# Weight columns taken 512 at a time in two projections, and a first chunk with its rounded products first

## The reference

```python
# first block, each of 2 layers
x = x + 0.5 * swiglu(rms_norm(x, ffn1_norm[l]), ffn1_w_gate[l], ffn1_w_up[l], ffn1_w_down[l])
h = rms_norm(x, mix_norm[l])
(nq, ..., wv, bgate) = jnp.split(h @ w_in[l], SPLIT_POINTS, axis=-1)     # 1024 x 5656
g = jax.nn.sigmoid(bgate).reshape(B, S, 3, D_MODEL)                      # last 3072 columns
merged = g[:, :, 0] * (y_nsa @ w_up_nsa[l]) + g[:, :, 1] * (y_sb @ w_up_sb[l]) + g[:, :, 2] * (y_swa @ w_up_swa[l])
# second block, each of 2 layers
q, k, v, r, a_low, u, v_sgu = split_proj(x @ w_in[l])                    # 1024 x 2576
```

## Time and profile before

| | |
|---|---|
| median of 3 runs | 2310.48 us (2309.97 to 2311.44) |
| the profiled execution | 2309.98 us |
| its span, first to last instruction | 2308.1 us |
| mean granted clock of PE | 0.994 |
| PE busy | 2266.3 us, 98% |
| DVE busy | 1599.9 us, 69% |
| ACT busy | 1243.4 us, 54% |

### The profile page before, as it was taken

One profiled execution on the slowest core, in us unless ns is written; L12 is line 12 of the kernel. 1 busy time (PEld: TensorE's weight loads), 2 busy tenths in 40 slices (PEclk: granted clock), 3 DMA queues, 4 the chain that ended last, 5 costly groups with the idle time before them and its releaser, 6 DMA issues.

```text
span 2308.1 us, 31674 instructions
## 1 busy us (share of the span) xinstructions
PE 2266.3 (98%) x13500; PEld 1971.8 (85%) x13500; DVE 1599.9 (69%) x1552; ACT 1243.4 (54%) x1272; POOL 48.1 (2%) x67
## 2 busy tenths in 40 slices
PE   8999999999999999999999999999999999899998
PEld 7888989788888899997888999888888998788886
DVE  6765845777477558557774656688887666688887
ACT  4434644454354346444443545577776545477775
POOL 1000100000000000000000000000000000000000
PEclk9999999999999999999999999999999999899999
DMA  7755443555556554535555554599998554599995
GB/s 229 219 190 170 143 148 129 164 183 192 191 172 193 182 165 134 159 132 182 183 189 191 171 177 165 178 341 348 369 345 278 180 183 148 193 346 344 348 367 188
DMA packets 309953, 490.96 MB, mean 213 GB/s; under 512 B 15504, under 2 KB 205120, under 8 KB 309808
## 3 DMA queue, kind: packets, MB, share of 16 engines
q1 hardware_dynamic: 305712, 475.35, 61.2%
q0 software_dynamic: 3104, 10.38, 1.6%
q10 hardware_dynamic: 992, 3.15, 0.4%
HBM read 487.40 MB, written 1.44 MB: 212 GB/s over the span
## 4 chain that ended last, share of the span: by engine, by line
PE 93%; DVE 4%; ACT 2%; issue 1%; DMA 0%; DVEq 0%; SPq 0%; ACTq 0%
PE PS L687 20%; PE PS L688 20%; PE PS L691 20%; PE PS L764 14%; PE PS L767 7%; PE PS L1388 1%; PE PS L991 1%; PE PS L956 1%; ACT RH L1557 1%; DVE RL L2057 1%; PE PS L930 1%; PE PS L941 1%; DVE X L2442 1%; PE PS L1353 1%; PE PS L1409 1%
## 5 line engine op out<-in xcount | busy, mean ns | idle before, releaser
L2057 DVE TENSOR_TENSOR RL<-RINGS,RH 128x2048 fp32r<-128x2048 f32 x448 | 1017.5, 2273 | 475.0 <-ACT RH L1557 472.5
L1557 ACT ACTIVATE RH<-RINGS 128x2048 fp32r<-128x2048 f32 x447 | 849.0, 1900 | 464.2 <-PE PS L691 449.5
L687 PE MATMUL PS<-RH,HTS 128*128 128x256 f32 (+1 forms) x1696 | 547.6, 334 | 0.4 <-DVE HTS L2039 0.4
L688 PE MATMUL PS<-RH,HTS 128*128 128x256 f32 (+1 forms) x1696 | 537.2, 328 | 0.0
L764 PE MATMUL PS<-HTS,RH 128*128 128x512 f32 x1384 | 416.8, 397 | 1.5 <-DVE HTS L2043 1.3
L691 PE MATMUL PS<-RL,HTS 128*128 128x256 f32 (+1 forms) x1696 | 400.9, 327 | 0.0
L687 PEld LDWEIGHTS PS<-RH,HTS 128*128 128x128 f32 x1696 | 319.8, 189 | 32.7 <-issue 2.5
L688 PEld LDWEIGHTS PS<-RH,HTS 128*128 128x128 f32 x1696 | 321.0, 189 | 27.9
L691 PEld LDWEIGHTS PS<-RL,HTS 128*128 128x128 f32 x1696 | 290.3, 189 | 31.1 <-DVE RL L2057 0.4
L764 PEld LDWEIGHTS PS<-HTS,RH 128*128 128x128 f32 x1384 | 248.6, 188 | 49.3 <-issue 1.6
L767 PE MATMUL PS<-HTS,RL 128*128 128x256 f32 x1408 | 285.4, 282 | 1.4 <-DVE RL L2057 1.4
(11 more groups left out here) (441 smaller groups left out, 2529.0 us busy)
## 6 DMA issues: line engine op xcount, KB each, us to landing
RINGS<-w_in SPq DMA_DIRECT2D x64, 1024.0 KB, 5.4
RINGS<-w_gate SPq DMA_DIRECT2D x64, 1024.0 KB, 5.4
RINGS<-w_up SPq DMA_DIRECT2D x64, 1024.0 KB, 5.6
RINGS<-w_down SPq DMA_DIRECT2D x64, 1024.0 KB, 5.4
RINGS<-ffn_w_up SPq DMA_DIRECT2D x44, 1024.0 KB, 5.4
RINGS<-ffn_w_down SPq DMA_DIRECT2D x44, 1024.0 KB, 4.9
RINGS<-ffn_w_gate SPq DMA_DIRECT2D x43, 1024.0 KB, 5.4
RINGS<-w_out SPq DMA_DIRECT2D x16, 1024.0 KB, 4.9
```

The costliest lines, as they stand in the source:

```text
L687: mm(dst, a_[0], b_[0], start=start, stop=False)
L688: mm(dst, a_[0], b_[1], start=False, stop=False) if left else mm(dst, a_[1], b_[0], start=False, stop=False)
L1557: A(splits.buffer(RH, RH3)[:, 0:width], RINGS[:, slot, 0:width], ACT.Copy).then_inc(wh_ready, 1)
L2057: TTn(RL[:, slot, 0:width], RINGS[:, slot, 0:width], splits.buffer(RH, RH3)[:, 0:width].bitcast(F32), ALU.subtract).then_inc(wl_ready, 1)
```

## The change

- Chunks 11 to 22 of the first mixer become six pairs. A load of a pair has four of the eight blocks of rows and 512 columns; the two loads of a pair add up in PSUM, half t = 1 of the rows in bank 1, half t = 0 in bank 0. Each load has 24 products of 512 columns (`to_wide_rows`), t = 1 first. ACT takes bank 0 in turn i when the pair is complete (even i), DVE bank 1 in the same turn, after a new semaphore `chunk_half` that PE raises when t = 1 of the second load is complete.
- Units 1 to 10 of the second block become five pairs in the same way.
- PE waits for bank 1 before the first load of a pair, and for bank 0 in the middle of it.
- In the first chunk of all, both parts' products with rounded weights (k = 0 to 6) come ahead of the wait for RL.

```diff
             for l in range(L):
                 swiglu(l, "ffn1")
                 for j in range(N1):
-                    cols(a["w_in"], l, OFF1[j], W1[j])
+                    if j < WIDE:
+                        cols(a["w_in"], l, OFF1[j], W1[j])
+                    else:
+                        half, c0 = (j - WIDE) % 2, OFF1[j - (j - WIDE) % 2]
+                        src = a["w_in"][l].rearrange("(k p) n -> p k n", p=P)[:, 4 * half:4 * half + 4, c0:c0 + 512]
+                        load(src, lambda r: r.rearrange("p (k n) -> p k n", n=512))
...
                         rounded_with_both(0, k)
+                    if opening:
+                        for k in range(K - 1):
+                            rounded_with_both(1, k)
                     pe.wait_ge(wl_ready, splits.v + splits.n)
                     for k in range(K):
                         rest_with_rounded(0, k)
                     rounded_with_both(0, K - 1)
+                if opening:
+                    for k in range(K):
+                        rest_with_rounded(1, k)
+                    rounded_with_both(1, K - 1).then_inc(chunks_done, 1)
+                    return
...
+            def to_wide_rows(half, lhs, between=None):
+
+                def items(wh, wl):
+                    wh, wl = (w.rearrange("p (k n) -> p k n", n=512) for w in (wh, wl))
+                    return [(PS[:, t, :], tuple(x[:, 4 * half + k, t * P:(t + 1) * P] for x in lhs), (wh[:, k, :], wl[:, k, :]),
+                             half + k == 0, half == 1 and k == 3, False) for t in (1, 0) for k in range(4)]
+                split_products(SLOT, 4, items, half=chunk_half if half else None, between=between)
...
                 for j in range(N1):
                     if j == 11:
                         pe.wait_ge(ng_cols, l + 1)
-                    elif j >= 2:
+                    elif j >= 2 and (j < WIDE or (j - WIDE) % 2 == 0):
                         col_taken(j - 2)
...
+                    elif (j - WIDE) % 2 == 0:
+                        to_wide_rows(0, HT, between=lambda: col_taken(j - 1))
                     else:
+                        to_wide_rows(1, HT, between=(lambda: transpose_y(tr1(l, 2), rows_src(0, l), 2)) if j == N1 - 1 else None)
...
                 def unit(i):
 
-                    if 2 <= i < 15:
+                    if i in (3, 5, 7, 9) or N2 <= i < 15:
                         taken(i - 2)
...
+                        elif i % 2:
+                            to_wide_rows(0, HT, between=(lambda: taken(i - 1)) if i > 1 else None)
                         else:
-                            to_rows(256, lambda t: bank, HT, at=256)
+                            to_wide_rows(1, HT)
...
             def take_unit(i):
+                if 0 < i < N2:
+                    c = min(COLS2[i - 1][0], COLS2[i][0])
+                    A(PROJ2[:, 0, c:c + 512], PS[:, 0, :], ACT.Copy).then_inc(unit_a, 1)
+                    return
...
                         split()
                     if i == 13 or i == 14:
                         ring.n += 2
+                    if i > WIDE and i % 2 == 0:
+                        dve.wait_ge(chunk_half, l * 8 + (i - WIDE + 1) // 2)
+                        TSc(PROJ[:, 1, OFF1[i - 1]:OFF1[i - 1] + 512], PS[:, 1, :], SMALL[:, 5:6], None, ALU.mult).then_inc(col_d, 1)
                     chunk()
...
                     split(WIDTH2[i + 2] if i < 15 else SLOT)
                     if i == 9:
                         ring.next()
+                    if i in (2, 4, 6, 8, 10):
+                        c = min(COLS2[i - 1][0], COLS2[i][0])
+                        dve.wait_ge(chunk_half, 8 * L + 5 * l + i // 2)
+                        V.tensor_copy(PROJ2[:, 1, c:c + 512], PS[:, 1, :]).then_inc(unit_d, 1)
                     chunk()
-                    if i % 2:
+                    if i % 2 and i >= N2:
                         take_unit(i)
```

More of the change, by code:

```diff
@@ L27 @@
 N1 = len(W1)
+WIDE = 11
 OFF1 = [sum(W1[:j]) for j in range(N1)]
@@ L369, in build @@
         branch_gates = sem("branch_gates")
-        up_half = sem("up_half")
+        chunk_half = sem("chunk_half")
         merged_rows = sem("merged_rows")
@@ L558, in _, with unit_columns @@
             for l in range(L):
-                for j in range(9):
-                    cols(a["w_in_2"], l, *COLS2[j])
+                def unit_columns(j):
+                    half, c0 = (j + 1) % 2, min(COLS2[j][0], COLS2[j + 1 if j % 2 else j - 1][0])
+                    src = a["w_in_2"][l].rearrange("(k p) n -> p k n", p=P)[:, 4 * half:4 * half + 4, c0:c0 + 512]
+                    load(src, lambda r: r.rearrange("p (k n) -> p k n", n=512))
+                cols(a["w_in_2"], l, *COLS2[0])
+                for j in range(1, 9):
+                    unit_columns(j)
                 load(a["w_s_2"][l].rearrange("g t s -> t g s"),
@@ L1001, in _ @@
                         to_few_columns(24, 1, HT)
-                    else:
-                        to_rows(W1[j], lambda t: j % 2 if j else 4, HT, at=256, ht=n if j == 0 else None,
-                                between=(lambda: transpose_y(tr1(l, 2), rows_src(0, l), 2)) if j == N1 - 1 else None)
+                    elif j < WIDE:
+                        to_rows(W1[j], lambda t: j % 2 if j else 4, HT, at=256, ht=n if j == 0 else None)
+                    elif (j - WIDE) % 2 == 0:
+                        to_wide_rows(0, HT, between=lambda: col_taken(j - 1))
+                    else:
+                        to_wide_rows(1, HT, between=(lambda: transpose_y(tr1(l, 2), rows_src(0, l), 2)) if j == N1 - 1 else None)
                     if 8 <= j < 8 + NU:
@@ L1129, in _ @@
                 col_taken(22)
-                rows_product(YT, 1, 0, k0=4, half=up_half)
+                rows_product(YT, 1, 0, k0=4, half=chunk_half)
                 pe.wait_ge(rows_taken, l + 1)
-                rows_product(YT, 1, 4, k0=6, half=up_half)
+                rows_product(YT, 1, 4, k0=6, half=chunk_half)
                 n = tr1(l, 3)
@@ L1176, in layer @@
                     if i == 3:
+                        taken(1)
                         taken(2)
@@ L1733, in _ @@
                     chunk()
-                    if i % 2 == 0:
+                    if i > WIDE and i % 2 == 0:
+                        A(PROJ[:, 0, OFF1[i - 1]:OFF1[i - 1] + 512], PS[:, 0, :], ACT.Copy, scale=SMALL[:, 4:5]).then_inc(col_a, 1)
+                    elif i % 2 == 0:
                         for t in range(T):
@@ L2348, in _ @@
                         V.tensor_copy(HS[0:24, 0, :], PS[0:24, 1, 0:S]).then_inc(ng_cols, 1)
-                    elif i % 2:
+                    elif i % 2 and i < WIDE:
                         w = W1[i]
@@ L2400, in summed @@
                     return TTn(dst[:, t, at:at + n], TMP[:, t, at:at + n], Y[:, t, at:at + n], ALU.add)
-                dve.wait_ge(up_half, 2 * l + 1)
+                dve.wait_ge(chunk_half, 8 * l + 7)
                 gated(0, low, 1)
@@ L2406, in _ @@
                 gated(1, low, 1)
-                dve.wait_ge(up_half, 2 * l + 2)
+                dve.wait_ge(chunk_half, 8 * l + 8)
                 gated(0, high, 2)
@@ L2502, in _ @@
                         dve.wait_ge(unit_d, units_d + 1)
+                        dve.wait_ge(unit_a, units_a + 2)
                         TTn(KDEC, PROJ2[:, :, GK:GK + 256], KEXP, ALU.mult).then_inc(kdec_ready, 1)
```

## The result

The changed kernel takes 2369.91 us in the median of 4 runs (2366.07 to 2371.21), the kernel before 2310.34. The ratio is 1.0258 (95% interval 1.0246 to 1.0270): 2.6% slower. The prediction was 2368.4, range 2345 to 2384. The profiled execution is the fastest of the four, 2366.07 us with a span of 2364.0.

A forecast was written before the change was run, and what follows sets the result against it. PE was taken as the bound (busy 98%, 93% of the last chain). Waits 42.3 + 5.1 and clock 20.9, less width 8.4 and opening 2.0, gave +57.9 us on 2310.48: 2368.4 us, range 2345 to 2384.

The forecast's parts named there:

- Part 2: Second block's pair ends: PE waits for DVE's copy of bank 1, queued behind the split; 42.3 us lost in two layers.
- Part 3: First mixer: DVE's take behind the split in turn 16 delays chunk 17; 5.1 us lost in two layers.
- Part 5: Clock halves behind the new waits: 1.9 us for each of ten, half for the mixer's two; 20.9 us lost.
- every wait above 3.07 us must cost: Second block: all ten waits exceed 3.07 us, a wait after which the clock was at 0.50; 1.9 us each.
- Part 1: 44 chunks in first mixer and second block: 24 wide products replace 48 narrow ones, 0.19 us each, 8.4 us saved.
- The formula that the prediction draws from the Trainium skill: Wide products: step is columns / 2.4 plus 2.5 ns, so 1056 merged pairs save 2.6 us; rival of negligible saving, chance 0.04.
- Part 4: First chunk: seven wide products fill the 1.38 us wait for RL; 2.0 us saved, bounds 0.8 and 2.1.

The follow-up runs named there:

- experiment 1: Changed kernel with DVE's take of bank 1 moved ahead of the split, in second block and first mixer: 2301.47 us, ratio 0.9966 to the kernel before.
- 7: Kernel with all takes early, but the first mixer's take in turns 14 and 16 put back behind the split: 2308.42 us, ratio 0.9998.
- Experiment 6: Changed kernel, copies still late, PE kept busy in the second block's ten waits by products nobody reads: 2349.23 us, ratio 1.0178.
- 2: Kernel with the early takes, each 512-column product in the pairs made as two of 256 columns: 2309.34 us, ratio 1.0002.
- experiment 3: Kernel before with the first chunk's new order alone: 2308.58 us, ratio 0.9998.

## Why the prediction was right

- **Part 2, who takes the results.** The step that decided. Forecast a layer: 4.0, 5.4, 5.2, 3.1 and 3.5 us, 42.3 in all. Measured in the changed kernel: 3.95, 5.29, 5.01, 3.25 and 3.23, 41.5 in all. What was shown beyond the numbers is the cause: with the take ahead of the split, ten waits come down to 1.1 us in sum (experiment 1).
- **Part 3, the mixer.** Forecast 5.1 us in two waits, measured 4.8; removed in experiment 1, alone in 7. In turn 14 no wait came, as forecast.
- **Part 5, the clock.** Forecast 20.9 us, 19.0 for the ten waits and 1.9 for the mixer's two. Behind the waits of the second block PE worked 18.7 us at half clock in the first layer (from the waits' ends to 1288.1, 1305.1, 1325.6 and 1363.2) and 18.2 in the second. Not half of that is lost, as the prediction had it, but 45%, since a wide product takes 0.427 us there and 0.235 at full clock: 16.6 us. Experiment 6 gives the same directly, 16.7 us between the starts of the same products. The form was rougher than the sum: I had each of the ten cost 1.9, but two cost nothing and the others 1.3 to 2.6, and that every wait above 3.07 us must cost was wrong. For the mixer's two I counted half; they cost nothing in one profile and about 1.5 us each in another. One more stretch at half clock, near 366 us, cost the changed kernel's profile 1.5 us that no new wait explains.
- **Part 1, the width.** Forecast 8.4 us, 0.19 a load. Measured 0.185 a load, 8.1 us, between experiments 1 and 2. Each load starts with a slow product, 0.1 us over the step, but at either width, so that cancels. Net it is 6.7 us there, because of the small waits that experiment 1 still has. One of them answers a remark of the prediction: with bank 1 free in time, ACT's take of bank 0 was to have 0.1 to 0.3 us to spare, and in unit 5 of each layer it had less than nothing. The formula that the prediction draws from the Trainium skill ("TensorE: Matmul & The Clock Gate", section "Back-to-back issue gap") is given in that section for a product by itself, beside about 131 ns as the spacing of 512-column products in a stream. The trace agrees with neither: 5.40 us for the 23 steps of a load is 0.235 us each.
- **Part 4, the opening.** Forecast 2.0 within 0.8 and 2.1. In the two profiles first compared it is 2.5, and that is the first execution's late clock; against other executions of the same kernel it is 0.7 to 0.9, and 0.9 by the medians of experiment 3. The mechanism (the wait is filled) held, but the greater part of the gain was one execution's.

The sum came within 1.5 us of the median, and that closeness is in part luck. The growth between the two profiles was 55.9 us, 2.0 below the forecast of 57.9: waits 1.1 and clock 2.7 too high (18.2 us with the stretch near 366), width 0.3 too high, opening 0.5 too low. These four add up to 53.9 us; of the 2.0 left, about 1.4 is that a start is delayed by some 0.1 us more than the row of the wait says, since the ends of products in the rows are modelled, and 0.6 is not assigned. The median then lies 3.8 us above the profiled execution, and no trace shows what those are made of. The accuracy of the sum is not better than that of its terms, some 3 us.

What stays open: which of two waits of the same length lets the clock fall. No run here tells them apart beforehand.

## What to carry to other kernels

When results are taken in larger units, ask in which order the engine that takes them does its work, not only when they are ready: a take queued behind work that waits for the end of that same unit can't be early, however soon its bank is full. Read it from three starts in the profile before (the producer's next start, the queued work's start, the length of both) and price the wait as their difference. Then look for the half clock behind each new wait; here it added four tenths of the ten longest waits themselves. And before you credit an edit with a change of the clock, profile the unchanged kernel once more.

## What the runs showed of the hardware

- Two waits of nearly equal length in one execution, 3.25 and 3.23 us, were followed by full clock and by 5.8 us at half clock; waits of 2.38 us by full clock in one kernel and by 3.2 us and more at half in another. The wait of 1.43 us at the end of the first mixer, which the prediction took as harmless from one execution, had a second of 0.67 us behind it, and in the third execution of the same kernel the clock was at 0.50 for 3.4 us from 422.0 on, right behind the two.
- Useless products in ten waits were worth 20.7 us of 2370 by the medians, of which the traces place 16.7 behind those waits.
- At half clock a product of 512 columns took 0.427 us from start to start, at full clock 0.235: 3.4 us at half clock lost about 1.5 us, not 1.7.
- The first step of a load behind products of another kind was 0.1 us longer than the others: 0.34 instead of 0.23 us at 512 columns in the changed kernel (1341.03), 0.22 instead of 0.12 at 256 in the kernel before (1278.75).
- The timed runs of the unchanged kernel spread from 2307.5 to 2311.4 us; its three profiles have the stretches at half clock in different places, and one such stretch shifts what follows by about 1.5 us.
